# A two-layer decoder step on one Trainium2 core: quartered first loads with two projection groups side by side, and output projections that begin before the attentions have ended

## What is computed

```python
# layer 0
h = x @ w_in                                  # "ab_in", 1024 -> 2048
y = concat(pool_mixer(u), retention(q, k, v, g)) @ w_o        # "ab_o"
# layer 1
q, k, v, f = x @ w_in                         # "fox_in"
y = forgetting_attention(q, k, v, f) @ w_o    # "fox_o": 16 heads of 64
# every layer
x = LN(alpha * x + y)
x = LN(alpha * x + memattn(x, mem))           # "mq", attention over 256 rows, 4 heads of 256, "mo"
x = LN(alpha * x + hier_moe(x))               # 16 experts, 2 per token
```

## Time and profile before

| | us |
|---|---|
| median of 3 runs | 1586.33 |
| the runs | 1583.40, 1586.33, 1597.59 |
| profiled execution, first to last instruction (span) | 1573.9 |
| median less span | 12.4 |
| TensorE matmuls busy | 1449.1 |
| VectorE busy | 566.1 |
| ScalarE busy | 322.6 |
| GpSimd busy | 217.1 |

### The profile page before, as it was taken

One profiled execution on the slowest core, in us unless ns is written; L12 is line 12 of the kernel. 1 busy time (PEld: TensorE's weight loads), 2 busy tenths in 40 slices (PEclk: granted clock), 3 DMA queues, 4 the chain that ended last, 5 costly groups with the idle time before them and its releaser, 6 DMA issues.

```text
span 1573.9 us, 21590 instructions
## 1 busy us (share of the span) xinstructions
PE 1449.1 (92%) x8463; PEld 967.5 (61%) x8463; DVE 566.1 (36%) x1203; ACT 322.6 (20%) x753; POOL 217.1 (14%) x249
## 2 busy tenths in 40 slices
PE   8999999999988999989999989989999984989990
PEld 6888888876765333357888864448875762323330
DVE  1631334433373111123533336753515165111115
ACT  0111211222041111114100035530223032111112
POOL 0000000000003333222410000000000002353354
PEclk9999999999999999999999999999999995999996
DMA  8211423454476999876358698942435255989963
GB/s 310 79 54 57 149 92 103 166 212 175 173 284 245 379 389 401 328 300 220 120 212 333 241 336 303 378 187 82 184 107 214 107 192 201 367 356 390 353 189 122
DMA packets 86286, 357.69 MB, mean 227 GB/s; under 512 B 23081, under 2 KB 26697, under 8 KB 59681
## 3 DMA queue, kind: packets, MB, share of 16 engines
q1 hardware_dynamic: 51376, 274.34, 45.7%
q0 software_dynamic: 24512, 46.99, 8.9%
q10 hardware_dynamic: 10297, 34.97, 5.6%
HBM read 408.17 MB, written 33.11 MB: 280 GB/s over the span
## 4 chain that ended last, share of the span: by engine, by line
PE 79%; DVE 8%; DMA 5%; issue 3%; ACT 2%; SPq 1%; POOL 0%; ACTq 0%; POOLq 0%; DVEq 0%
PE PS L640 75%; DMA MKV<-in_moe_w_gu,OVR 2%; PE PS L1192 2%; DMA W<-in_fox_v 1%; DVE EX L1273 1%; DMA O<-in_moe_w_down,OVR 1%; SPq L511 1%; PE PS L727 1%; DMA X<-in_x 1%; SPq L512 1%; PE PS L1214 1%; ACT X L1950 1%; DMA y_rows<-BIG 0%; PE PS L969 0%; DVE TOK L1872 0%
## 5 line engine op out<-in xcount | busy, mean ns | idle before, releaser
L640 PE MATMUL PS<-X,W 128*128 128x260 f32 x1264 | 288.9, 386 | 11.6 <-DMA W<-in_ab_w_in 6.5
L640 PEld LDWEIGHTS PS<-X,W 128*128 128x128 f32 x1264 | 239.1, 191 | 52.1 <-issue 10.5
L640 PE MATMUL PS<-O,W 128*128 128x260 f32 x1024 | 228.8, 383 | 2.4 <-DVE O L1658 1.6
L640 PEld LDWEIGHTS PS<-O,W 128*128 128x128 f32 x1024 | 193.7, 190 | 36.9 <-issue 3.4
L1888 ACT ACTIVATE BIG<-PS 128x512 f32<-128x512 f32 (+2 forms) x161 | 75.0, 467 | 306.0 <-PE PS L640 186.9
L640 PE MATMUL PS<-W,BIG 128*64 128x512 f32 x512 | 115.1, 603 | 2.0 <-DVE BIG L1791 2.0
L2365 POOL TENSOR_TENSOR SM<-SM,O 128x5 f32<-128x5 f32 x2 | 0.4, 194 | 791.5 <-DVE SM L1736 791.5
L1796 DVE SCALAR_TENSOR_TENSOR BIG<-BIG,SM,PS 128x256 f32<-128x256 f32 x32 | 15.4, 480 | 244.1 <-ACT BIG L2228 244.1
L640 PE MATMUL PS<-MKV,BIG 128*64 128x512 f32 (+1 forms) x384 | 91.4, 525 | 1.4 <-ACT BIG L1888 1.0
L1266 DVE SCALAR_TENSOR_TENSOR X<-X,PS 128x260 f32<-128x260 f32 x64 | 27.1, 423 | 152.6 <-PE PS L640 152.6
L640 PEld LDWEIGHTS PS<-W,BIG 128*64 128x64 f32 x512 | 36.5, 139 | 69.5 <-issue 69.5
(11 more groups left out here) (329 smaller groups left out, 1758.8 us busy)
## 6 DMA issues: line engine op xcount, KB each, us to landing
W<-in_moe_w_gu SPq DMA_DIRECT2D x64, 1024.0 KB
TMP<-in_moe_w_down SPq DMA_DIRECT2D x32, 1024.0 KB
W<-in_fox_kt SPq DMA_DIRECT2D x64, 512.0 KB, 5.9
W<-in_fox_v SPq DMA_DIRECT2D x64, 512.0 KB, 6.5
W<-in_mem_kt SPq DMA_DIRECT2D x16, 1024.0 KB, 8.9
W<-in_cache_mem_v SPq DMA_DIRECT2D x16, 1024.0 KB, 8.8
y_rows<-BIG ACTq DMA_DIRECT2D x32, 512.0 KB
W<-in_mem_wkv SPq DMA_DIRECT2D x13, 1024.0 KB, 4.8
```

Of the source, the lines that this page charges most:

```text
L640: return nc.tensor.matmul(out, lhsT, rhs, start=start, stop=stop, **kw)
```

## The change

1. Start: the loads of `X` half 0 and of block 0 are cut from halves to quarters (two k tiles each; eight DMAs where there were four), each pair on a semaphore `ld_first0` to `ld_first3` (the last weight part on `w_in0`). The order of `ab_in` begins (0, 0), (1, 0), (0, 1), (1, 1), so the first two groups both use half 0, and PE runs them side by side, two k tiles of each per quarter (`first_groups`). `ld_x1` is waited for at the third group. DVE clears two banks first and the other six after.
2. `fox_o`: 7 of 8 k tiles of group 0 are issued in step v = 31, of group 1 in step 32 and of group 2 after the loop; the banks are 0, 2, 3, 1 in turn. What is left of the three (one k tile each) follows after `ready_fox`.
3. `mo`, in both layers: 6 of 8 k tiles of group 0 are issued at u = 18, before the last `values`, and of group 1 after it; the banks are 2, 3, 0, 1 in turn. The rest of group 0 stands before `sample_values(0)`, that of group 1 between it and `sample_collect(0)`.

```diff
--- before.py
+++ after.py
@@ -42,7 +42,7 @@
     if kind == "seven":
         return [(0, 0), (0, 1), (1, 0), (1, 1)] + [(2 * b + m, h) for b in range(1, tiles // 2) for m, h in ((0, 0), (1, 1), (1, 0), (0, 1))]
     if kind == "wide":
-        return [(m, h) for m in range(tiles) for h in range(2)]
+        return [(0, 0), (1, 0), (0, 1), (1, 1)] + [(m, h) for m in range(2, tiles) for h in range(2)]
     if kind == "halved":
         return [(m, h) for h in range(2) for m in range(tiles)]
     return [(m, 0) for m in range(tiles)]
@@ -83,6 +83,10 @@
         for g, (name, m, h) in enumerate(self.seq):
             pos = g - self.start[name]
             b = pos % 2 if beside_retention(name, pos) else pos % 4
+            if name == "fox_o":
+                b = (0, 2, 3, 1)[pos % 4]
+            if name in ("mo0", "mo1"):
+                b = (2, 3, 0, 1)[pos % 4]
             if name == "fox_in" and pos >= 4:
                 b = (3 * (pos // 4 % 2), 2, 1, 2)[pos % 4]
             self.bank.append(b)
@@ -435,6 +439,8 @@
             w = Wl[PROJ.slot[PROJ.block0["fox_in"] + b]]
             return w[:, 0:4, 0:P], w[:, 4:8, 0:P], w[:, 0:4, P:2 * P], w[:, 4:8, P:2 * P]
 
+        FIRST_PARTS = KT // 2
+
         block = ctx.enter_context(nc.Block())
 
         FIRST1 = PROJ.block0["kv1"] + EARLY // 2
@@ -548,11 +554,15 @@
 
             for l in range(2):
                 if l == 0:
-                    half = KT // 2 * BW
-                    sp.dma_start(X[:, 0:4, 0:HALF], a["x"][:, 0, 0:4]).then_inc(S("ld_first"), 16)
-                    sp.dma_start(W[:, 0, 0:half], w_src["ab_in"][0][:, 0:half]).then_inc(S("ld_first"), 16)
-                    sp.dma_start(X[:, 4:8, 0:HALF], a["x"][:, 0, 4:8]).then_inc(S("ld_x0"), 16)
-                    sp.dma_start(W[:, 0, half:2 * half], w_src["ab_in"][0][:, half:2 * half]).then_inc(S("w_in0"), 16)
+                    for n in range(FIRST_PARTS):
+                        k = slice(2 * n, 2 * n + 2)
+                        cols = slice(2 * n * BW, (2 * n + 2) * BW)
+                        sp.dma_start(X[:, k, 0:HALF], a["x"][:, 0, k]).then_inc(S(f"ld_first{n}"), 16)
+                        w_part = sp.dma_start(W[:, 0, cols], w_src["ab_in"][0][:, cols])
+                        if n < FIRST_PARTS - 1:
+                            w_part.then_inc(S(f"ld_first{n}"), 16)
+                        else:
+                            w_part.then_inc(S("w_in0"), 16)
                     sp.dma_start(X[:, :, HALF:T], a["x"][:, 1]).then_inc(S("ld_x1"), 16)
                     load(1)
                     sp.dma_start(CS[:, :], a["const"]).then_inc(S("ld_const"), 16)
@@ -639,31 +649,40 @@
             def mm(out, lhsT, rhs, start=True, stop=True, **kw):
                 return nc.tensor.matmul(out, lhsT, rhs, start=start, stop=stop, **kw)
 
-            def group(name, pos, src, n=HALF):
+            def group(name, pos, src, n=HALF, part=range(KT)):
                 g, m, h = PROJ.groups(name)[pos]
-                if g:
-                    pe.wait_ge(*arrived(PROJ.block0[name] + m // 2))
-                else:
-                    pe.wait_ge(S("ld_first"), 32)
-                if PROJ.prev[g] is not None:
-                    wait_evac(pe, PROJ.count[PROJ.prev[g]])
+                if part[0] == 0:
+                    if g >= 2:
+                        pe.wait_ge(*arrived(PROJ.block0[name] + m // 2))
+                    if PROJ.prev[g] is not None:
+                        wait_evac(pe, PROJ.count[PROJ.prev[g]])
                 w = Wl[PROJ.slot[PROJ.block0[name] + m // 2]]
                 b = bank(PROJ.bank[g])
-                for k in range(KT):
-                    if g == 0 and k == KT // 2:
-                        pe.wait_ge(S("ld_x0"), 16)
-                        pe.wait_ge(S("w_in0"), 16)
+                for k in part:
                     if name in ("kv0", "kv1") and m >= 8:
                         last = mm(b[:, 0:BW], src[:, k, (m % 2) * P:(m % 2 + 1) * P], w[:, k, :], k == 0, k == KT - 1)
                     else:
                         last = mm(b[:, 0:n], w[:, k, (m % 2) * P:(m % 2 + 1) * P],
                                   src[:, k, h * HALF:h * HALF + n], k == 0, k == KT - 1)
-                last.then_inc(S("proj_acc"), 1)
-
-            def proj(name, src, ready, hooks={}, n=HALF, until=None):
+                if part[-1] == KT - 1:
+                    last.then_inc(S("proj_acc"), 1)
+
+            def first_groups():
+
+                for i in range(FIRST_PARTS):
+                    if i < FIRST_PARTS - 1:
+                        pe.wait_ge(S(f"ld_first{i}"), 32)
+                    else:
+                        pe.wait_ge(S(f"ld_first{i}"), 16)
+                        pe.wait_ge(S("w_in0"), 16)
+                    for pos in range(2):
+                        group("ab_in", pos, X, part=range(2 * i, 2 * i + 2))
+
+            def proj(name, src, ready, hooks={}, n=HALF, until=None, begun={}):
                 for pos, (g, m, h) in list(enumerate(PROJ.groups(name)))[:until]:
                     ready(m, h, pos)
-                    group(name, pos, src, n)
+                    if begun.get(pos, 0) < KT:
+                        group(name, pos, src, n, range(begun.get(pos, 0), KT))
                     if pos in hooks:
                         hooks[pos]()
 
@@ -800,10 +819,16 @@
                 for f in steps:
                     f()
 
+            def ready_abin(m, h, pos):
+                if pos == 2:
+                    pe.wait_ge(S("ld_x1"), 16)
+                    pe.wait_ge(S("ps_zero"), 2)
+
             pe.wait_ge(S("ps_zero"), 1)
-            proj("ab_in", X, lambda m, h, pos: pe.wait_ge(S("ld_x1"), 16) if pos == 1 else None,
+            first_groups()
+            proj("ab_in", X, ready_abin,
                  {7: windows, 13: lambda: mix_pool(0), 14: lambda: mix_pool(1), 15: lambda: mix_pool(2), 16: lambda: mix_pool(3),
-                  20: lambda: key_rows(0), 21: lambda: key_rows(1), 22: lambda: key_rows(2), 23: lambda: key_rows(3)}, until=24)
+                  20: lambda: key_rows(0), 21: lambda: key_rows(1), 22: lambda: key_rows(2), 23: lambda: key_rows(3)}, until=24, begun={0: KT, 1: KT})
 
             beside(1)
             wait_out(pe, "ab_in", None, range(12))
@@ -1021,13 +1046,19 @@
                             values((v - 5) // 4)
                         if v in hooks:
                             hooks[v]()
+                        if v == 31:
+                            pe.wait_ge(S("fa_out"), 7)
+                            group("fox_o", 0, O, part=range(KT - 1))
+                        if v == 32:
+                            pe.wait_ge(S("sa_out"), 4)
+                            group("fox_o", 1, O, part=range(KT - 1))
+                    group("fox_o", 2, O, part=range(KT - 1))
 
                     def ready_fox(m, h, pos):
                         if pos == 0:
                             pe.wait_ge(S("fa_out"), 8)
                             pe.wait_ge(S("fa_p"), 64)
-                            pe.wait_ge(S("sa_out"), 4)
-                    proj("fox_o", O, ready_fox, ln_hooks(4, "fox_o", 0, 9, 12))
+                    proj("fox_o", O, ready_fox, ln_hooks(4, "fox_o", 0, 9, 12), begun={0: KT - 1, 1: KT - 1, 2: KT - 1})
 
 
                 qi = 4 * l
@@ -1111,6 +1142,12 @@
                         values(u // 4 - 2)
                     if u in hooks:
                         hooks[u]()
+                    if u == 18:
+                        pe.wait_ge(S("ma_out"), 8 * l + 6)
+                        pe.wait_ge(S("s_weights"), 5 * l + 2)
+                        group(f"mo{l}", 0, O, part=range(KT - 2))
+                pe.wait_ge(S("s_turned"), 5 * l + 1)
+                group(f"mo{l}", 1, O, part=range(KT - 2))
 
                 def ready_mo(m, h, pos):
                     if pos == 0:
@@ -1119,7 +1156,7 @@
                     if pos == 8:
                         pe.wait_ge(S("sa_out"), 4 * l + 2)
                 proj(f"mo{l}", O, ready_mo, {0: lambda: sample_values(0), 1: lambda: sample_collect(0), 4: lambda: sample_values(1), 5: lambda: sample_collect(1),
-                                             **ln_hooks(qi + 2, f"mo{l}", 0, 9, 13)})
+                                             **ln_hooks(qi + 2, f"mo{l}", 0, 9, 13)}, begun={0: KT - 2, 1: KT - 2})
 
                 def parts(h):
                     for n in range(2):
@@ -1442,7 +1479,8 @@
                 put_sample(bank(6), s_)
 
 
-            V.memset(bank(0, 8), 0.0).then_inc(S("ps_zero"), 1)
+            V.memset(bank(0, 2), 0.0).then_inc(S("ps_zero"), 1)
+            V.memset(bank(2, 6), 0.0).then_inc(S("ps_zero"), 1)
             V.memset(QPAIR, 0.0)
             link(V.memset(QM, 0.0))
             V.memset(U[:, :, 0:16], 0.0).then_inc(S("u_pad"), 1)
```

## The result

Twenty runs of each kernel on one chip: 1578.35 us after the change (1573.63 to 1587.74) and 1587.49 before (1579.58 to 1597.59). The ratio is 0.9948, its 95% interval 0.9932 to 0.9964: 5.7 to 10.8 us faster, about half a per cent. The forecast was 1579.3.

What follows compares the result with a forecast made beforehand. The prediction took TensorE, with matmuls for 92% of the span, as the bound, so only its gaps could be won: 2.7 + 3.5 + 0.8 = 7.0 us off the median 1586.33 gives 1579.3, range 1572.5 to 1588.

Steps and rivals of the forecast that it cites:

- rival (c): All three places gain their upper bounds, 3.55 + 3.63 + 2 x 1.31 = 9.8 us, giving 1576.5; chance 0.08.
- The start, 2.7: At the first projection, quartered loads let the third group begin at 13.75 instead of 16.45 us, gaining 2.7 us.
- so bytes and not issues set its landing: At the start, half 1 of X still lands at 12.9 us despite four more issues, since the queue is full.
- Rival (a): The start gains only 1.2 us, as four extra issues delay half 1 to 15.2; total 5.5, 1580.8; chance 0.13.
- The forgetting attention, 3.5: At its end, early output projection work fills TensorE's gaps; 3.8 us worked out, 3.5 taken after cost of turns.
- the bound of 3.63: Most the end of the forgetting attention could gain: its gaps of 2.10, 0.74 and 0.79 us.
- The memory attentions, 2 x 0.4: At both layers' ends, gaps of 0.53 and 0.78 shrink, a 0.56 us wait on the pick appears; 0.4 net each.
- (d): Slower: TensorE's clock falls in layer 0's router too; 7.0 us of matmuls there cancel the gain, 14 give 1593.3; chance 0.04.
- The sum, 7.0: Whole kernel: 2.7 + 3.5 + 0.8 = 7.0 us gained, a span of 1566.9 and a time of 1579.3.
- The 12.4 us around the span: Whole kernel: span before 1573.9, median of runs 1586.33; the 7.0 us gain was set against that median.
- its own signs: Wrong if a stretch outside the three places changes over 2 us, or first experts or router show a clock below 1.
- Rival (b): Attention gains are lost waiting for overflow weights at the last mixture of experts; only the start counts, 1583.6; chance 0.10.

Runs made afterwards that it cites:

- e4: The changed kernel with its first loads in halves again, the two groups still side by side: 1580.08 us, ratio to before 0.997.
- e2: The kernel before with only part 2 of the change (early output projection in the forgetting attention): 1578.95 us, ratio to before 0.9968.
- e5: The changed kernel with first loads of 2, 2 and 4 tiles and three, not six, early group 1 tiles in `mo`: 1576.73 us, ratio to before 0.9943.
- the parts alone: Three kernels, each the kernel before with one of the change's three parts only: -2.7, -5.1 and +1.6 us.
- the second measurement: The changed kernel, unaltered, measured again beside the kernel before on another chip: 1578.96 us, ratio 0.9928.
- e1: The changed kernel without parts 2 and 3, so only the new start against the kernel before: 1580.68 us, ratio to before 0.9983.
- e8: The changed kernel with a projection group moved between the halves of each of two narrow matmul stretches in layer 0's retention: 1576.89 us, ratio to before 0.993.
- e9: The changed kernel with the edits of e5, e7 and e8 together: 1567.26 us, ratio to before 0.9896.
- e10: e9 with six more unused matmuls per layer around the experts' first gathered rows and their transposes: 1568.38 us, ratio to before 0.9907.
- e7: The changed kernel with 48 matmuls of unused result added to layer 1's router: 1575.67 us, ratio to before 0.9922.

## Why the prediction was right

The forecast, 1579.3, is 0.95 us from the measured median. The mechanism held: TensorE was the bound, its gaps could be filled, and the largest gain is where the largest term had it. That the number came so close is in part luck. The median of three runs from which the 7.0 us were taken, 1586.33, was 1.2 us below the median of twenty, and the gain was 9.1 us by the medians, 2.1 more than forecast and nearer to the 9.8 of rival (c); the two errors cancel in part. The forecast of the span, 1566.9, was missed: it measured 1572.6. By its steps:

- **The start, 2.7: measured 2.45 in the first profile, 2.0 in the mean** of five quartered against three unchanged starts. The begin (4.97, measured 5.11), the 32 instructions without a gap and the third group (13.75, measured 13.96) came as worked out. One step failed in part: that the queue is full, "so bytes and not issues set its landing". Half 1 landed at 13.9 and not 12.9. Rival (a) had 15.2, so it was right by less than half. Table by stage of after, whose last number, GB/s, was 358 and 373 in the same windows before:

```profile
4.00:6.00 2.00, 0.89 (x2) 0.83 (x3) 1.74 (x4) 0.00 (x0) 0.00 (x0) 1.00 0.94 260
6.00:8.00 2.00, 2.00 (x6) 1.52 (x6) 0.00 (x0) 0.00 (x0) 0.00 (x0) 1.00 0.94 242
```

  The DMA engines are nearly as busy (0.94; 1.03 and 1.05 before) and move two thirds of the bytes, while the quarters are in flight. The bytes missing over these 4 us are worth about the microsecond, so it is put down to the smaller pieces and not to the issues; no run changes the one without the other. In e4, with halves, it is 371 and 399. The advice for large DMAs in the Trainium skill, "DMA: Bandwidth & Descriptors", "Rules for kernel authors", points the right way, and the trace agrees in sign. The figure for one DMA that the prediction took from the same page, and did not use, stands there for DMAs issued by GpSimd, and these are SyncE's: the first weight quarter, near 4.0 by it, landed 3.6 us after its issue at 1.37, at 5.0.
- **The forgetting attention, 3.5: measured 3.96 at full clock, about 5.2 in the mean.** Its part alone (e2) is the only one whose ratio excludes 1. That the blocks would come in time, with 3 us of cover, held. The step that failed is the bound of 3.63, the sum of the gaps. A gap counts from a modelled end, and the next work can start before that end. By starts, each step of the earlier trace rows less the same step in e5 (the first, 1054.22 to 1054.88, stands ahead of the rows shown), the three gaps are 2.93 - 0.66, 1.80 - 0.87 and 3.17 - 2.30, 4.07 us; my 3.8, cut to 3.5 for the turns, was nearer before the cut. And the price of a gap was taken as its length, though in two of the three profiles with the gaps the clock fell behind them.
- **The memory attentions, 2 x 0.4: measured 2 x 0.64 ahead and 2 x -0.8 behind, net nothing or a small loss.** The row says 0.33 for the new wait and not 0.56, but it counts from a modelled end. The pick began 0.14 us after `sample_values` and took 1.28, as forecast, and from the four instructions to the next it is 1.48 us by starts where they need 0.89: 0.59 lost. The gain ahead is larger than 0.4 since the gap before the projection was worth 1.05 us by starts (4.48 from the last `values` to what follows, now 3.43) and not 0.78. The step that failed is that nothing behind the pick was priced: the load of the next sample's values was late in some layers, and the clock fell in four of twelve, where a dense group no longer stands between two narrow kinds. The rival for that, (d), looked for it in the router, and for gaps. Its sentence that the change "makes none over 0.6 us", and so keeps the clock, was the wrong test: no gap there was over 0.34 us, and in the retention the clock fell without any.
- **The sum, 7.0.** In the mean of the profiles it is 2.0 + 5.2 - 2 x 0.17 = 6.9 by place; the parts alone add to 6.2; the first measurement says 5.7 to 10.8, the second (0.9904 to 0.9952) 7.6 to 15.2. So 7.0 came out about right by place, with one term too small and two too large, and below the second measurement. Whether the 1 to 4 us more that the times show come from elsewhere or are the scatter of the clock stays open.
- **The 12.4 us around the span** were in truth 1.7, and the rest was the one profiled execution, 10 us below the mean of the 75. It did no harm because the gain was taken from the median of the runs; had I set the sum against a run like the profiled one, it would have been 10 us too low.
- **Rival (d)** shows in small: in after's layer 0 router the clock is 0.87 in 490 to 500 us, where before's profile has 1.00, and the first gate-up matmul takes 8.90 and not 7.09 us. But e1, whose router is before's, shows 0.66 there. After's second profile has 7.09 us there again. It is scatter, which the change neither makes nor cures, and it hid most of the gain between the two spans. By its own signs the prediction would be wrong here: it named a clock below 1 at the first router and a stretch outside the three places that changes by over 2 us, and both came, 0.87 and 3.2 us. The signs were ill chosen, since one profile against one can't tell the change from the scatter, which is what the prediction had said of the clock itself. The Trainium skill, "TensorE: Matmul & The Clock Gate", Part 1, says that the moment of the rise differs between runs; the starts of after and e1 agree, with some six and some thirteen slow instructions for the same code. What the 75 runs of before add is the size: they span 22 us, more than twice the change's gain.
- **Rival (b)** (given back at the expert weights) is ruled out: that wait is 7.2 us in two times, 6.8 before. **Rival (c)** needed the pick covered and half 1 on time; e5 has the first, and half 1 at 13.3 and not 12.9. The places rule it out; the times alone don't.

## What to carry to other kernels

Where an engine is 92% busy, its few gaps can be priced one by one, and filling them with parts of the next stage that are ready gives their length and here somewhat more; count what stood between two awkward pieces before taking it away. Work out a gap from start to start, against the same steps without one, and ask what the clock does behind it. Compare places, not spans: read the granted clock beside every duration, and ask whether the one profile is a typical run before its distance to the median is used. Between two stretches of narrow matmuls a dense group kept the clock up here.

## What was unexpected of the hardware

- The granted clock fell with TensorE busy all the time. Behind 64 float32 matmuls of 8 x 64 weights and 128 columns (4.3 us) and behind 32 with two output columns (4.4 us) it was 0.64 and 0.79, and four groups took 9.88 + 9.70 = 19.6 us for the 4 x 3.72 = 14.9 of full speed. With one group between their halves it stayed at 1.00 in the profiles of e8, e9 and e10. Only the order was changed for that; how narrow is too narrow was not tried.
- Idle time bought speed back: with 20 us of matmuls whose results nobody reads layer 1's router stretch was shorter (42.93, 42.39 and 42.32 us in e7, e9 and e10, against 44.7 to 46.6 in the nine others).
- The first matmuls are slow by different counts. After's start fits some six instructions at the slow step, e1's some thirteen (its windows begin at 35.99), with the same code: 1 us of scatter in the start alone. The tables by stage print a granted clock of 1.00 in these windows all the same, so that the slow step there is the lower clock is read from the pace (0.433 us against 0.2215) and not from the clock's own row.
- Between 4 and 8 us, where the first loads are in flight, five profiles with pieces of 256 and 260 KB moved 233 to 299 GB/s with the DMA engines 0.85 to 0.96 busy, and four with pieces of 512 and 520 KB 352 to 399 with 1.00 to 1.06.
